# The high and low parts of a split input, moved into two regions of SBUF

## The chip, the cores and the metric

The kernel runs on one core of a Trainium2 chip. Its time is the device time of one execution in microseconds (us); lower is better. Five engines work beside each other in a core: TensorE (PE, matmuls; its weight loads are shown apart as PEld), VectorE (DVE), ScalarE (ACT), GpSimd (POOL) and SyncE (SP, which issues DMAs here). SBUF is the memory that they share, 128 partitions wide.

## The reference

Two blocks of a transformer over 256 tokens of width 1024, in float32. The first has two layers, each with a feed-forward part, an attention mixer, another feed-forward part and a gate; the second has a convolution and delta-rule mixer and 32 experts. The part that the change bears on is the input of the feed-forward parts and of two input products:

```python
def rms_norm(x, g):
    y = xf * lax.rsqrt(jnp.mean(xf * xf, axis=-1, keepdims=True) + EPS)
    return (y * g.astype(jnp.float32)).astype(x.dtype)

def swiglu(x, w_in, w_out):
    gate, up = jnp.split(x @ w_in, 2, axis=-1)
    return (jax.nn.silu(gate) * up) @ w_out

for i in range(DEPTH):                                     # DEPTH = 2
    h = h + FFN_HALF * swiglu(rms_norm(h, g_ffn1[i]), ffn1_w_in[i], ffn1_w_out[i])
    ...
    h = h + FFN_HALF * swiglu(rms_norm(h, g_ffn2[i]), ffn2_w_in[i], ffn2_w_out[i])
```

The hidden width of a feed-forward part is 2816, which is 22 chunks of 128.

## The kernel before

Features lie on the partitions: an activation of width 1024 is 8 tiles (index k) of 128 features by 256 tokens (T = 256). Weights stream in from HBM in chunks of 24 tiles of 128x128 through a ring of four buffers.

The dense products keep float32 accuracy with a faster type. Weights and inputs are each split into a high part, rounded to float32r, and a low part, the rest, and a product is three matmuls: high by high, high weights by low input, low weights by high input. ScalarE makes the high weights (`high`, or `high_first` for a stage's first chunk; L1563), VectorE the low ones (`ring_lo`, L2050). For the input, ScalarE writes `x_hi` (`x_high_pair`, L1574) and VectorE `x_lo` (`x_low_pair`, L2079), tile by tile, as soon as the residual stream `h` has its new value. Both are views of one tensor, `x_parts`:

```python
x_parts = inside(rounded_view("x_parts", [P, 2 * KD * T + LINE]), [P, KD, 2, T])
x_hi, x_lo = x_parts[:, :, 0, :], x_parts[:, :, 1, :]
```

In a partition the order is high k=0, low k=0, high k=1, low k=1 and so on, 256 elements each. `inside` starts a view 15 elements (INSIDE) into its tensor, which is 60 bytes behind a multiple of 64; every run of 256 elements of 4 bytes then starts at 60 bytes inside a group of 64. The tensor lies over `hn` and `sq`, which are used at other times. The hidden activations `act_hi` and `act_lo`, two tensors of their own, start 60 bytes inside as well.

Who reads `x_parts`:
- The four feed-forward stages (`gated`; `ffn1_0`, `ffn2_0`, `ffn1_1`, `ffn2_1`). For each of the 22 chunks, gate and up have 8 tiles each. Since high and low of one k are neighbours, one matmul of 512 columns multiplies a high weight with both and puts the results beside each other in a PSUM bank; one of 256 columns multiplies the low weight with `x_hi`. `gate_up` first issues the 16 of 512 columns and then the 16 of 256; `first_gate_up` goes by k, for the stage's first chunk, and waits for each k's low part. The down product of the chunk before, 24 matmuls of 256 columns from `act_hi` and `act_lo`, follows.
- The input product of the second block (`mix_in`): three matmuls of 256 columns for each tile, `x_hi` and then `x_lo` with the high weight, `x_hi` with the low one.
- The input product of the fox mixer (`two_units`), where 128 columns of `x_hi` or `x_lo` are the stationary operand and 512 columns of weights stream by.

All matmuls but the experts' go through the helper at L587. The order on TensorE is the order of the code; other engines are waited for by semaphores. The last quarter of the kernel, the experts, streams its weights from HBM and reads none of `x_parts`.

Of the kernel before, what the change touches and what calls it, by code (L numbers as in the profile page):

```python
# [14 lines left out]
P = 128  # L15
T = 256
D = 1024
KD = D // P
# [23 lines left out]
LINE = 16  # L42
INSIDE = 15
# [154 lines left out]
def two_block_kernel(nc, xT, pT, pos, par, weights, experts, out):  # L198
    with ExitStack() as ctx:
# [3 lines left out]
        def rounded_view(name, shape):  # L203

            with nc.sbuf_tensor("sb_" + name, shape, F32R) as view:
                return view

        def inside(flat, shape):

            n = math.prod(shape[1:])  # L210
            names = "abc"[:len(shape) - 1]
            dims = {a: shape[1 + i] for i, a in enumerate(names)}
            return flat[:, INSIDE:INSIDE + n].rearrange(f"p ({' '.join(names)}) -> p {' '.join(names)}", **dims)
# [23 lines left out]
        v_tok = sb("v_tok", [P, 2, D])  # L237
        oT = sb("oT", [P, KD, T])
        h = sb("h", [P, KD, T])
        x_parts = inside(rounded_view("x_parts", [P, 2 * KD * T + LINE]), [P, KD, 2, T])  # L240
        x_hi, x_lo = x_parts[:, :, 0, :], x_parts[:, :, 1, :]
        hn = sb("hn", [P, KD, T])
        sb("behind_hn", [P, LINE])
        sq = sb("sq", [P, KD, T])
# [338 lines left out]
        def _(pe):  # L583
# [92 lines left out]
            def gated(name):  # L676
# [3 lines left out]
                def product(bank, slot, part, k, inc=None):  # L680

                    w_hi, w_lo = split_tile(slot, 2 * k + part)
                    mm(bank[:, :], w_hi, x_parts[:, k, :, :].rearrange("p a t -> p (a t)"), k == 0, False)
                    mm(bank[:, 0:T], w_lo, x_hi[:, k, :], False, k == KD - 1, inc)

                def gate_up(slot, par):

                    banks = (GATE[par], UP[par])
                    for part, bank in enumerate(banks):
                        for k in range(KD):  # L690
                            w_hi, _ = split_tile(slot, part * KD + k)
                            mm(bank[:, :], w_hi, x_parts[:, k, :, :].rearrange("p a t -> p (a t)"), k == 0, False)
                    for part, bank in enumerate(banks):
                        for k in range(KD):
                            _, w_lo = split_tile(slot, part * KD + k)
                            mm(bank[:, 0:T], w_lo, x_hi[:, k, :], False, k == KD - 1,
                               gu_ready if part and k == KD - 1 else None)
# [2394 lines left out]
```

## Time and profile before

| | us |
|---|---|
| median of three executions | 1721.98 |
| lowest, highest | 1719.61, 1722.22 |
| the profiled execution | 1720.82 |
| its span, first to last instruction | 1719.0 |
| TensorE busy in the span | 1615.6 (94%) |
| VectorE, ScalarE, GpSimd busy | 987.5, 610.3, 57.4 |

The granted TensorE clock had a mean of 0.989 of full speed. A matmul's record ends some time after the next one has started, since matmuls are pipelined: the time that one takes of the engine is the distance from its start to the next one's, and not the mean duration in its row. Where a row merges several matmuls, the distance is the time from the row's start to the next row's, divided by their number.

### The profile page before, as it was taken

What the parts mean: (1) busy time and instruction counts of PE and PEld (TensorE: products, weight loads), DVE (VectorE), ACT (ScalarE), POOL (GpSimd) and SP (SyncE); (2) the same over time, 40 slices, a digit from 0 to 9 for tenths busy, and PEclk for the clock granted to TensorE, in tenths of its full rate; (3) what the DMA queues carried; (4) which work ended last, traced back from release to release, by engine and by line L of the source; (5) the groups of instructions that cost most, each with busy time, mean ns of one, the idle gap of its engine ahead of it and who ended that gap; (6) DMA issues with size and microseconds to landing.
All of it is one profiled execution on the core that took longest, in us unless ns stands there. A gap on an engine that the chain in (4) does not pass through costs nothing.

```text
span 1719.0 us, 25786 instructions
## 1 busy us (share of the span) xinstructions
PE 1615.6 (94%) x10376; PEld 1286.3 (75%) x10376; DVE 987.5 (57%) x1660; ACT 610.3 (36%) x809; POOL 57.4 (3%) x82
## 2 busy tenths in 40 slices
PE   7999999999999999999999999999989888788867
PEld 6999857899998999888889999999854444334423
DVE  7888655688767788865487885788331111111112
ACT  5333346434336333465543334653421000000001
POOL 4000005000000000001100000000000000000000
PEclk9999999999999999999999999999989999999999
DMA  7555442555554555544255555343699999999996
GB/s 282 191 183 183 184 184 74 184 184 188 194 232 160 195 198 190 190 153 173 74 191 195 197 187 212 120 147 124 240 375 426 426 426 427 428 427 428 427 427 245
DMA packets 49530, 415.68 MB, mean 242 GB/s; under 512 B 5648, under 2 KB 5680, under 8 KB 8368
## 3 DMA queue, kind: packets, MB, share of 16 engines
q1 hardware_dynamic: 49392, 414.61, 61.5%
q8 instruction: 53, 0.87, 0.2%
q14 instruction: 21, 0.17, 0.0%
q10 hardware_dynamic: 64, 0.03, 0.0%
HBM read 413.54 MB, written 1.05 MB: 241 GB/s over the span
## 4 chain that ended last, share of the span: by engine, by line
PE 74%; DMA 18%; DVE 4%; ACT 3%; issue 1%; SPq 0%; POOL 0%; DVEq 0%; ACTq 0%
PE bank L587 66%; DMA sb_moe_ring<-experts 17%; PE bank L1281 7%; DVE sb_ring_lo L2050 1%; ACT sb_high L1563 1%; DMA sb_ring<-weights 1%; PE bank L776 0%; PE bank L865 0%; DMA sb_h<-xT 0%; SPq L513 0%; DVE sb_x_parts L2079 0%; ACT sb_high_first L1563 0%; DVE sb_nmax L2183 0%; DVE sb_lnv L2086 0%; ACT sb_x_parts L1574 0%
## 5 line engine op out<-in xcount | busy, mean ns | idle before, releaser
L2050 DVE TENSOR_TENSOR sb_ring_lo<-sb_ring,sb_high 128x2304 fp32r<-128x2304 f32 (+4 forms) x180 | 351.9, 1956 | 123.5 <-ACT sb_high L1563 122.9
L587 PE MATMUL bank<-sb_x_parts,sb_high 128*128 128x512 f32 (+1 forms) x1792 | 407.5, 365 | 0.3 <-DVE sb_ring_lo L2050 0.2
L587 PEld LDWEIGHTS bank<-sb_x_parts,sb_high 128*128 128x128 f32 x1792 | 317.8, 189 | 49.4 <-DVE sb_ring_lo L2050 0.8
L1563 ACT ACTIVATE sb_high<-sb_ring 128x3072 fp32r<-128x3072 f32 x100 | 274.9, 2748 | 139.6 <-PE bank L587 111.0
L587 PE MATMUL bank<-sb_x_parts,sb_ring_lo 128*128 128x256 f32 x1632 | 253.0, 279 | 0.0
L587 PEld LDWEIGHTS bank<-sb_x_parts,sb_ring_lo 128*128 128x128 f32 x1632 | 224.5, 189 | 7.0
L587 PE MATMUL bank<-sb_act_hi,sb_ring_lo 128*128 128x256 f32 x704 | 195.0, 277 | 0.0
L587 PE MATMUL bank<-sb_act_hi,sb_high 128*128 128x256 f32 x680 | 188.6, 277 | 2.2 <-DVE sb_ring_lo L2050 1.7
L587 PE MATMUL bank<-sb_act_lo,sb_high 128*128 128x256 f32 x680 | 187.7, 276 | 0.0
L1605 ACT ACTIVATE sb_expg<-sb_gate_r 128x256 f32<-128x256 f32 x88 | 36.7, 418 | 338.0 <-DVE sb_gate_r L2113 337.9
L1281 PE MATMUL bank<-sb_moe_ring,sb_act 128*32 128x512 f32 x464 | 118.3, 640 | 38.1 <-DMA sb_moe_ring<-experts 38.1
L1281 PE MATMUL bank<-sb_moe_ring,sb_sq 128*32 128x512 f32 x960 | 115.5, 604 | 32.7 <-DMA sb_moe_ring<-experts 32.1
L587 PE MATMUL bank<-sb_oT,sb_ring 128*128 128x256 f32 x640 | 142.8, 379 | 0.0
L587 PEld LDWEIGHTS bank<-sb_oT,sb_ring 128*128 128x128 f32 x640 | 120.7, 190 | 16.7 <-issue 0.8
L587 PEld LDWEIGHTS bank<-sb_act_hi,sb_ring_lo 128*128 128x128 f32 x704 | 131.7, 187 | 0.0
L587 PEld LDWEIGHTS bank<-sb_act_hi,sb_high 128*128 128x128 f32 x680 | 127.2, 187 | 2.6 <-DVE sb_ring_lo L2050 1.9
L587 PEld LDWEIGHTS bank<-sb_act_lo,sb_high 128*128 128x128 f32 x680 | 127.2, 187 | 0.0
L1281 PEld LDWEIGHTS bank<-sb_moe_ring,sb_act 128*32 128x32 f32 x464 | 31.1, 116 | 108.9 <-issue 108.2
L2838 DVE TENSOR_TENSOR sb_act<-bank,sb_expg 128x128 f32<-128x128 f32 x32 | 9.3, 291 | 162.1 <-ACT sb_expg L1991 162.1
L1281 PEld LDWEIGHTS bank<-sb_moe_ring,sb_sq 128*32 128x32 f32 x960 | 27.8, 109 | 97.5 <-issue 94.0
L2833 DVE COPY sb_sq<-bank 128x512 f32<-128x512 f32 x32 | 22.1, 691 | 131.8 <-PE bank L1281 131.8
L1281 PEld LDWEIGHTS bank<-sb_stack,sb_sq 128*128 128x128 f32 x512 | 59.6, 191 | 29.7 <-issue 29.7
(395 smaller groups left out, 1922.7 us busy)
## 6 DMA issues: line engine op xcount, KB each, us to landing
sb_ring<-weights SPq DMA_DIRECT2D x133, 1536.0 KB, 6.5
sb_moe_ring<-experts SPq DMA_DIRECT2D x176, 1024.0 KB, 21.9
sb_qk<-experts SPq DMA_DIRECT2D x8, 1024.0 KB, 17.9
sb_front<-experts SPq DMA_DIRECT2D x2, 1024.0 KB, 13.2
sb_oT<-experts SPq DMA_DIRECT2D x2, 1024.0 KB, 17.6
sb_moe_ring<-experts SPq DMA_DIRECT2D x8, 256.0 KB, 19.1
sb_front<-experts SPq DMA_DIRECT2D x2, 768.0 KB, 14.2
sb_h<-xT SPq DMA_DIRECT2D x2, 512.0 KB, 6.6
```

Source lines behind the costliest of these rows:

```text
L587: ins = nc.tensor.matmul(o, l, r, start=start, stop=stop, skip_group_check=True)
L1281: ins = nc.tensor.matmul(o, l, r, start=start, stop=stop, skip_group_check=True)
L1563: nc.scalar.activation(high_of(n)[:, lo * P:hi * P], ring[:, n % RING, lo * P:hi * P], ACT.Copy).then_inc(done, 1)
L1605: nc.scalar.activation(expg[:, b, :], gate_r[:, b, :], ACT.Silu).then_inc(sig_ready, 1)
L2050: return V.tensor_tensor(ring_lo[:, n % RING, cols], ring[:, n % RING, cols], high_of(n)[:, cols].bitcast(F32), ALU.subtract)
L2833: V.tensor_copy(partial[:, 1, :], B[1][:, :]).then_inc(part_in[1], 1)
L2838: V.tensor_tensor(a3, turned_part(1), s3_, ALU.mult).then_inc(ex_act, 1)
```

## The change

High and low parts get a region each inside `x_parts`. The high region has the eight tiles of `x_hi` behind each other, starting at element 15; the low region has those of `x_lo`, starting at element 15 + 2049 = 2064 = 129 x 16, a multiple of 64 bytes. Two neighbours of one k are now 2049 elements apart. The matmuls of 512 columns read them as two runs of 256, [2049, 2] by [1, 256]; what they write in PSUM is the same 512 columns. The tensor is 16 elements longer. What ScalarE and VectorE write, and all waits, stay as they were; the number of instructions is the same on every engine.

```diff
-        x_parts = inside(rounded_view("x_parts", [P, 2 * KD * T + LINE]), [P, KD, 2, T])
-        x_hi, x_lo = x_parts[:, :, 0, :], x_parts[:, :, 1, :]
+        x_run = KD * T + LINE - INSIDE
+        x_both = rounded_view("x_parts", [P, 2 * KD * T + 2 * LINE])[:, INSIDE:INSIDE + 2 * x_run]
+        x_parts = x_both.rearrange("p (a n) -> p a n", a=2)[:, :, 0:KD * T].rearrange("p a (k t) -> p a k t", t=T)
+        x_hi, x_lo = x_parts[:, 0, :, :], x_parts[:, 1, :, :]
...
                 def product(bank, slot, part, k, inc=None):
-                    mm(bank[:, :], w_hi, x_parts[:, k, :, :].rearrange("p a t -> p (a t)"), k == 0, False)
+                    mm(bank[:, :].rearrange("p (a t) -> p a t", a=2), w_hi, x_parts[:, :, k, :], k == 0, False)
...
                 def gate_up(slot, par):
-                            mm(bank[:, :], w_hi, x_parts[:, k, :, :].rearrange("p a t -> p (a t)"), k == 0, False)
+                            mm(bank[:, :].rearrange("p (a t) -> p a t", a=2), w_hi, x_parts[:, :, k, :], k == 0, False)
```

## Rows read from the trace of the kernel before

**Rows 1.** Page: the span, TensorE's busy time, the chain's shares.

```profile
span 1719.0 us, 25786 instructions
...
PE 1615.6 (94%) x10376; PEld 1286.3 (75%) x10376; DVE 987.5 (57%) x1660; ACT 610.3 (36%) x809; POOL 57.4 (3%) x82
...
PE bank L587 66%; DMA sb_moe_ring<-experts 17%; PE bank L1281 7%; DVE sb_ring_lo L2050 1%; ACT sb_high L1563 1%; DMA sb_ring<-weights 1%; PE bank L776 0%; PE bank L865 0%; DMA sb_h<-xT 0%; SPq L513 0%; DVE sb_x_parts L2079 0%; ACT sb_high_first L1563 0%; DVE sb_nmax L2183 0%; DVE sb_lnv L2086 0%; ACT sb_x_parts L1574 0%
```

**Rows 2.** Windows: stretch, busy time and instructions by engine, granted clock, DMA.

```profile
546.00:706.00 160.00, 159.37 (x1071) 146.90 (x1071) 129.62 (x176) 62.37 (x44) 0.00 (x0) 1.00 0.51 188
...
865.00:1050.00 185.00, 184.81 (x1236) 170.30 (x1236) 146.65 (x202) 72.82 (x59) 0.00 (x0) 1.00 0.53 194
...
1093.00:1208.00 115.00, 115.00 (x958) 111.72 (x958) 97.58 (x161) 61.26 (x67) 0.00 (x0) 1.00 0.35 129
```

**Rows 3.** Waits of TensorE: who waited for whom, total us, times, longest.

```profile
PE bank L1281 <- DMA sb_moe_ring<-experts: 70.1, 42, 3.0
PE bank L587 <- DVE sb_ring_lo L2050: 13.6, 3, 11.7
```

**Rows 4.** Groups by shape, moving operand named first: busy us, mean ns of one.

```profile
L587 PE MATMUL bank<-sb_x_parts,sb_high 128*128 128x512 f32 x1344 | 322.4, 391 | 0.3 <-DVE sb_ring_lo L2050 0.2
...
L587 PE MATMUL bank<-sb_x_parts,sb_high 128*128 128x256 f32 x448 | 85.1, 288 | 0.1
...
L587 PE MATMUL bank<-sb_x_parts,sb_high_first 128*128 128x512 f32 x64 | 26.4, 445 | 11.8 <-DVE sb_ring_lo L2050 11.7
```

**Rows 5.** Timeline of TensorE, a turn of ffn1_1's loop: start us, us, operation.

```profile
603.70 0.28 PE L587 MATMUL bank<-sb_act_hi,sb_high 128*128 128x256 f32 x1
...
606.47 3.83 PE L587 MATMUL bank<-sb_x_parts,sb_high 128*128 128x512 f32 x16
610.14 2.03 PE L587 MATMUL bank<-sb_x_parts,sb_ring_lo 128*128 128x256 f32 x16
612.01 0.28 PE L587 MATMUL bank<-sb_act_hi,sb_high 128*128 128x256 f32 x1
...
614.78 3.83 PE L587 MATMUL bank<-sb_x_parts,sb_high 128*128 128x512 f32 x16
```

**Rows 6.** Timeline of TensorE in the fox mixer, weights as the moving operand.

```profile
759.33 0.39 PE L587 MATMUL bank<-sb_ring_lo,sb_x_parts 128*128 128x512 f32 x1
...
768.99 0.39 PE L587 MATMUL bank<-sb_ring_lo,sb_x_parts 128*128 128x512 f32 x1
```

**Rows 7.** Timeline in the attention, around the mask's matmul.

```profile
279.77 0.92 PE L587 MATMUL bank<-sb_qk 96*128 96x128 f32 x4
...
280.34 0.47 PE L587 MATMUL bank<-sb_mask_r,sb_ident_r 128*128 128x256 f32 x1
```

**Rows 8.** Timeline of the input product of the second block, 14 groups of three.

```profile
1130.77 0.28 PE L587 MATMUL bank<-sb_x_parts,sb_ring_lo 128*128 128x256 f32 x1
...
1135.71 0.28 PE L587 MATMUL bank<-sb_x_parts,sb_ring_lo 128*128 128x256 f32 x1
```

**Rows 9.** All that touches `x_parts`: ns min/median/max; who waited, us and times.

```profile
L587 PEld LDWEIGHTS bank<-sb_high,sb_x_parts x168: 187/187/192, 740.1 to 806.3; 128*128 128x128 f32 x168
...
  PEld bank L587: 1.0, 3
```

**Rows 10.** Writers of `x_parts` and the same operations into aligned tensors, by shape.

```profile
L1574 ACT ACTIVATE sb_x_parts<-sb_h,sb_params 128x256 fp32r<-128x256 f32 x48 | 21.2, 495 | 11.4 <-DMA sb_h<-xT 5.6 <-DVE sb_h L2043 3.5 <-DVE sb_h L2227 2.3
L1656 ACT ACTIVATE sb_oT<-sb_h,sb_params 128x256 f32<-128x256 f32 x16 | 6.6, 497 | 5.4 <-DVE sb_h L2043 5.4
...
L2079 DVE SCALAR_TENSOR_TENSOR sb_x_parts<-sb_h,sb_params,sb_x_parts 128x256 fp32r<-128x256 f32 x48 | 20.8, 479 | 12.5 <-ACT sb_x_parts L1574 12.5
L2515 DVE SCALAR_TENSOR_TENSOR sb_qk<-sb_attn,sb_params,sb_qk 128x256 f32<-128x256 f32 x36 | 15.9, 482 | 0.6
```

## The prediction, made before the changed kernel ran

> **What bounds the kernel now.** I read the header and the shares of the chain first, then the waits of TensorE, then the windows by stage, and only then single instructions. TensorE is busy 94% of a span of 1719.0 us, and 66% of the chain that ended last is one line, the helper L587 through which every product outside the experts goes [rows 1]. Between 546 and 706 us it is busy 159.37 of 160 us, between 865 and 1050 us 184.81 of 185, and in the mixer's input product 115.00 of 115 [rows 2]. So in the dense stages nothing is waited for: of all TensorE waits on L587 the largest is 13.6 us in three places, and they are waits for split weights, which the change doesn't touch [rows 3]. Behind the dense stages the chain is the experts' DMA (17% of it), which reads none of the inputs that move. The change gives TensorE no work and takes none; it alters where its streamed operand lies. Hence only one question carries the forecast: does the spacing of the matmuls that read the moved operand change, by how many ns, times how many of them.
>
> **How many.** Four feed-forward stages with 22 chunks of 16 products each: 4 x 22 x 16 = 1408 matmuls of 512 columns stream high and low in one instruction. The profile has all of them, 1344 against weights in the high buffers and 64 against the first chunks' [rows 4]. One nanosecond on each is 1.4 us. A difference of 0.2%, about what a measurement of this kernel can tell from no change, is 3.4 us, or 2.4 ns on each of the 1408. Besides these, 224 products of the mixer's input read the low part alone, as the second of three matmuls of 256 columns (448 with high weights, of which half read low), and the fox mixer has x as its stationary operand.
>
> **How fast they go now.** In one turn of the loop 16 such matmuls start at 606.47 and the next group at 610.14: 3.67 / 16 = 229.4 ns. The following 16 of 256 columns take (612.01 - 610.14) / 16 = 116.9 ns each, and the 24 of the down product (606.47 - 603.70) / 24 = 115.4 ns [rows 5]. The granted clock is 1.00 throughout, the upper level of 2.4 GHz [rows 2], so no part of this is the clock. All of these start 60 bytes inside a group of 64. For an aligned start there is a row too: in the fox stage weights stream and x is stationary, 42 matmuls of 512 columns in 768.99 - 759.33 = 9.66 us, 230.0 ns [rows 6]. The two kinds of start are 0.6 ns apart, and the aligned one is the slower. Where a run starts is thus a small thing here.
>
> **Part 1: the jump.** After the change the 512 columns are two runs of 256 with a step of 2049 elements between them. High ends after 15 elements of its last group, low begins a new one. Counted in groups of 64 bytes, before it was elements 15 to 526, 33 groups; now 15 to 270, 17 groups, plus 16 for low, 33 again. If what such a matmul pays beside its columns goes with groups, nothing changes. No row shows a jump between two runs of this size, so I bound it. From above: a jump can hardly cost more than ending one matmul and starting another, which is also a jump, and comes with a new weight load. Two matmuls of 256 columns take 2 x 116.9 = 233.8 ns or 2 x 115.4 = 230.8 ns against 229.4 in one, so 4.4 or 1.4 ns; x 1408 = 6.2 or 2.0 us [rows 5]. The only matmul that streams two runs is the mask's (2 x 128 columns, the same 128 twice, and a split output as well): the products ahead of it end at 279.77 + 0.92 = 280.69, it ends at 280.34 + 0.47 = 280.81, so about 120 ns for 256 columns [rows 7], within the rounding of these rows of the 115 to 117 without a jump. From below: the low run now starts on a group, which for a whole matmul is 0.6 ns slower, not faster; a gain would have to come from the parting of high and low, which is weighed as a rival below. I take the value nearest to a row of the same size, the aligned run's: + 0.6 ns x 1408 = + 0.8 us, and keep 0 to + 6.2 us.
>
> The Trainium skill ("TensorE: Matmul & The Clock Gate", Back-to-back issue gap) puts a fixed 2.5 ns on every matmul beside its columns. If a jump cost such a start, an estimate by that page is 1408 x 2.5 = + 3.5 us instead of + 0.8; the rows give 1.4 to 4.4 ns for a start here, so they agree in size, but neither says that a jump is one. For a whole matmul the page gives 512 / 2.4 + 2.5 = 215.7 ns, and the trace differs: 229.4. The skill ("SBUF — State Buffer", Door 1: The DMA port swizzle) also says that full bandwidth needs at least two hits on a 16-byte line, which would favour aligned starts; the rows disagree, 230.0 ns aligned against 229.4 ns 60 bytes in.
>
> **Part 2: low read alone.** The mixer's groups of three go at (1135.71 - 1130.77) / 14 = 352.9 ns [rows 8], the down product's, whose high and low lie in tensors far apart, at 8 groups in 2.77 us = 346.2 ns [rows 5]. The same three shapes, 6.6 ns apart. If that comes from high and low being 1024 bytes apart in one region, separate regions give 224 x 6.6 ns = 1.5 us back; if not, nothing, or the 0.6 ns of an aligned start, + 0.1 us. I take the middle, - 0.7 us.
>
> **Part 3: the fox mixer.** A third of its weight loads now read low from an aligned address. Those loads (187 ns each) [rows 9] lie beside 512 columns of 230.0 ns, so the stream sets the pace. Nothing; if the cover were gone I would see it in the 230.0.
>
> **Part 4: the writers.** ScalarE writes the high part, 48 times 495 ns at 60 bytes inside a group; the same operation and scale into an aligned tensor takes 497 ns. VectorE's low part takes 479 ns, its sister into an aligned tensor 482 [rows 10]. The low write gets aligned and high loses its gaps: at most 48 x 3 ns = 0.1 us, most of it behind TensorE. Where TensorE waited for the low part it was 1.0 us in three places [rows 9], so even there it is noise. No instruction, semaphore or DMA is added, so no queue gets anything new behind it. Nothing.
>
> **Sum.** + 0.8 - 0.7 = + 0.1 us against the profiled execution's own 1720.8 us (span 1719.0 and 1.8 around it). That execution is 1.2 us under the median of three, 1722.0, so the forecast is 1722.1 us; the three runs themselves reach from 1719.6 to 1722.2.
>
> **The rivals.**
> A jump is a start: the stream stops at the end of the high run and is set up again, 1.4 to 4.4 ns, middle 2.9, x 1408 = + 4.1 us, 1726.1 us (1724.0 to 1728.2). For it: such a price is what every matmul pays now. Against it: part of that price may be the weights' change, and the mask's row shows nothing of it. It decides the verdict from 2.4 ns a matmul on. This is the slower side.
> What costs the mixer 6.6 ns in each of its threes is that high and low are neighbours, and it is in the 512 columns too, which read the same neighbours: 6.6 ns x 1408 = - 9.3 us, 1712.7 us. For it: both read the same bytes. Against it: a stream of 512 weights without such neighbours goes no faster, 230.0 ns, and in the mixer the cost may lie in the change from one run to the other and not in either.
> Only the mixer gains: - 1.5 us and a free jump, 1720.5 us. It is a shade of the forecast and ends as no change.
> A jump costs much more than a start, over 5 ns, above 1729 us: for it only that no row has such a jump.
> That the change doesn't do what it says, say a matmul cut into two, can be left out: the program of the changed kernel has as many TensorE instructions as before, with the two runs as one operand.
>
> **How the numbers follow.** Forecast, with the shade: 0.62. A start per jump: 0.25, a fifth of it below the 3.4 us that can be told apart. A gain in the 512 columns: 0.09. Much more than a start: 0.04. Faster 0.09; slower 0.20 + 0.04 = 0.24; within 0.2%: 0.67. The range takes in the start per jump at its upper end, 1728.2, and below it the mixer's gain and the spread of the runs, to 1718.8.
>
> **What would show it.** In the changed profile: the group of x with high weights, 128x512, x1344, busy 322.4 us now. It is 84 groups of 16, so each ns of spacing adds 84 x 15 ns = 1.3 us to it: about 323 if I am right, 326 if a jump is a start, 314 if the neighbours were to blame. One loop turn is 8.31 us from 606.47 to 614.78 and should stay within 0.02; a start per jump makes it 8.36. The mixer's three should stand between 346 and 353 ns. The fox stage's 230.0 ns, the writers' 495 and 479 ns should stand still. If the span moves while all of these stand, my premise that only the spacing matters is wrong.

## The result and the profile after

The changed kernel takes 1723.1 us (median of 22 executions, 1720.95 to 1725.08), the kernel before 1720.6 us in the same sessions (22 executions, 1718.31 to 1723.19). The ratio is 1.0014, 95% interval 1.0007 to 1.002: 2.5 us slower. That is small but clear of the spread, and it stays within the 0.2% named in the prediction. The time forecast was 1722.1 us. The profiled execution of after took 1723.0 us with a span of 1721.3.

The page of after, header and busy times (compare [rows 1]; lines from the change on stand two further down, so L587 is now L589):

```profile
span 1721.3 us, 25786 instructions
...
PE 1620.0 (94%) x10376; PEld 1287.1 (75%) x10376; DVE 987.7 (57%) x1660; ACT 610.5 (35%) x809; POOL 57.3 (3%) x82
...
PE bank L589 66%; DMA sb_moe_ring<-experts 17%; PE bank L1283 7%; DVE sb_ring_lo L2052 1%; ACT sb_high L1565 1%; DMA sb_ring<-weights 1%; PE bank L778 0%; PE bank L867 0%; DMA sb_h<-xT 0%; SPq L515 0%; DVE sb_x_parts L2081 0%; ACT sb_high_first L1565 0%; DVE sb_nmax L2185 0%; DVE sb_lnv L2088 0%; ACT sb_x_parts L1576 0%
```

As many instructions and as many matmuls as before, but TensorE is busy 4.4 us longer (1615.6 to 1620.0), and the chain has the same shape. The stages are as gapless as in [rows 2], at the same granted clock of 1.00 (stretch, busy time and instructions by engine, clock, DMA):

```profile
546.00:706.00 160.00, 159.14 (x1057) 145.16 (x1057) 128.92 (x175) 63.59 (x45) 0.00 (x0) 1.00 0.52 192
865.00:1050.00 185.00, 184.77 (x1234) 168.94 (x1233) 146.69 (x203) 72.95 (x60) 0.00 (x0) 1.00 0.52 191
```

The groups by shape, busy us and mean ns of one, say which matmuls (compare [rows 4]; the second group, low weights by the high part of the input, was 253.0 us before):

```profile
L589 PE MATMUL bank<-sb_x_parts,sb_high 128*128 128x512 f32 x1344 | 324.7, 393 | 0.3 <-DVE sb_ring_lo L2052 0.2
L589 PE MATMUL bank<-sb_x_parts,sb_ring_lo 128*128 128x256 f32 x1632 | 254.4, 280 | 0.0
```

322.4 has become 324.7, about midway between the 323 of the forecast and the 326 of the rival "a jump is a start". The turn of the loop shows the spacing (TensorE's timeline: start us, us, operation; compare [rows 5]):

```profile
603.69 2.04 PE L589 MATMUL bank<-sb_x_parts,sb_ring_lo 128*128 128x256 f32 x16
605.57 0.28 PE L589 MATMUL bank<-sb_act_hi,sb_high 128*128 128x256 f32 x1
...
608.34 3.86 PE L589 MATMUL bank<-sb_x_parts,sb_high 128*128 128x512 f32 x16
612.04 2.04 PE L589 MATMUL bank<-sb_x_parts,sb_ring_lo 128*128 128x256 f32 x16
```

The 16 matmuls of 512 columns take 3.70 us, 231.3 ns each (229.4 before). The 16 of 256 columns take 605.57 - 603.69 = 1.88 us, 117.5 ns each (116.9 before). The down product, which reads other tensors, still takes 2.77 us. The turn is 8.35 us where it was 8.31; the prediction had named at most 0.02 us of change for the forecast and 8.36 us for a start per jump, so by this sign the trace stood nearer to the rival. Rows are rounded to 10 ns; the mean distance of starts over all such matmuls in the trace is finer, and is what the rest of this text uses where it gives hundredths:

| start to start, ns | before | after | difference x count |
|---|---|---|---|
| 512 columns, high weights | 229.56 | 231.21 | +1.65 x 1408 = +2.3 us |
| 256 columns, low weights | 116.61 | 117.54 | +0.93 x 1408 = +1.3 us |
| mixer, group of three | 353.1 | 353.6 | +0.5 x 224 = +0.1 us |
| fox mixer, weights stream | 230.2 | 231.1 | +1.0 x 288 = +0.3 us, not clear of the spread |
| down product | 115.56 | 115.55 | 0 |

The fox mixer's row is weak: two executions of one and the same kernel further down, in which `x_parts` lies as before, have 230.2 and 230.8 ns there. With it the sum is +4.0 us, without it +3.7. From the first matmul to the last of the second block's input product the profiles have 1202.1 us before and 1205.8 after, +3.7. Of that 0.45 lies ahead of the first down product, where the spacing explains less than 0.1 (32 matmuls of each kind), and the stretch from `ffn1_0` to `ffn2_0`, with the attention in it, gives 0.34 back. Apart from such shifts at the edges of stages, which the spacing doesn't explain, the dense part lost what the spacing says: 0.040 us in every turn of the loops. The medians of the whole kernel lie 2.5 us apart, with 3.4 as the upper end of their interval, and the profile of before spends 1.6 us more on the experts than that of after. That last difference is between two single executions and says nothing about the change.

### The profile page after: what moved, and what is told of

Read it like the earlier page. It is cut to its first block, busy times and chain, and to the rows that moved or that the text cites. A ratio compares the mean times of both kernels' runs of the same rounds, so it can differ in the third digit from the quotient of the medians.

```text
span 1721.3 us, 25786 instructions
## 1 busy us (share of the span) xinstructions
PE 1620.0 (94%) x10376; PEld 1287.1 (75%) x10376; DVE 987.7 (57%) x1660; ACT 610.5 (35%) x809; POOL 57.3 (3%) x82
## 4 chain that ended last, share of the span: by engine, by line
PE 74%; DMA 18%; DVE 4%; ACT 3%; issue 1%; SPq 0%; POOL 0%; DVEq 0%; ACTq 0%
PE bank L589 66%; DMA sb_moe_ring<-experts 17%; PE bank L1283 7%; DVE sb_ring_lo L2052 1%; ACT sb_high L1565 1%; DMA sb_ring<-weights 1%; PE bank L778 0%; PE bank L867 0%; DMA sb_h<-xT 0%; SPq L515 0%; DVE sb_x_parts L2081 0%; ACT sb_high_first L1565 0%; DVE sb_nmax L2185 0%; DVE sb_lnv L2088 0%; ACT sb_x_parts L1576 0%
## 5 line engine op out<-in xcount | busy, mean ns | idle before, releaser
L589 PE MATMUL bank<-sb_x_parts,sb_high 128*128 128x512 f32 (+1 forms) x1792 | 409.9, 367 | 0.3 <-DVE sb_ring_lo L2052 0.2
L589 PEld LDWEIGHTS bank<-sb_x_parts,sb_high 128*128 128x128 f32 x1792 | 316.5, 188 | 53.0 <-DVE sb_ring_lo L2052 0.7
L589 PE MATMUL bank<-sb_x_parts,sb_ring_lo 128*128 128x256 f32 x1632 | 254.4, 280 | 0.0
L589 PEld LDWEIGHTS bank<-sb_x_parts,sb_ring_lo 128*128 128x128 f32 x1632 | 225.3, 190 | 7.2
L589 PE MATMUL bank<-sb_act_hi,sb_ring_lo 128*128 128x256 f32 x704 | 195.2, 277 | 0.0
L589 PE MATMUL bank<-sb_act_hi,sb_high 128*128 128x256 f32 x680 | 188.7, 277 | 2.2 <-DVE sb_ring_lo L2052 1.7
L589 PE MATMUL bank<-sb_act_lo,sb_high 128*128 128x256 f32 x680 | 187.9, 276 | 0.0
L589 PE MATMUL bank<-sb_oT,sb_ring 128*128 128x256 f32 x640 | 142.8, 380 | 0.0
L589 PEld LDWEIGHTS bank<-sb_oT,sb_ring 128*128 128x128 f32 x640 | 120.9, 190 | 16.4 <-issue 0.8
L589 PEld LDWEIGHTS bank<-sb_act_hi,sb_ring_lo 128*128 128x128 f32 x704 | 131.9, 187 | 0.0
L589 PEld LDWEIGHTS bank<-sb_act_hi,sb_high 128*128 128x128 f32 x680 | 127.6, 188 | 2.5 <-DVE sb_ring_lo L2052 1.9
L589 PEld LDWEIGHTS bank<-sb_act_lo,sb_high 128*128 128x128 f32 x680 | 127.4, 187 | 0.0
```

The costliest lines, as they stand in the source:

```text
L589: ins = nc.tensor.matmul(o, l, r, start=start, stop=stop, skip_group_check=True)
```

## The experiments

Four kernels, the streams, leave out the whole computation and do nothing but matmuls: 64 on each line of code, 16 weight tiles in turn, moving operands at the places of the kernels, one line after the other with no wait. (In the lines of code shown, the last argument, the flags that begin and end a sum, is left out.) A line's start subtracted from the next line's, divided by 64, is the time of one matmul. The other eight are whole kernels.

### The layouts alone, nothing beside them

Among the lines of `e1_streams_quiet` (in the run all lines stood two further down than the text on record says, so "before" is L429 and so on):

```python
M(whole(i), W(i), one(15 + 512 * k))         # L429: before
M(split(i), W(i), two(15 + 256 * k, 2049))   # L430: after
M(split(i), W(i), two(15 + 256 * k, 2064))   # L431: both runs 60 bytes inside
M(whole(i), W(i), one(512 * k))              # L432: one run of 512, aligned
M(split(i), W(i), two(256 * k, 2064))        # L433: both runs aligned
M(whole(i), W(i), one(15 + 256 * k))         # L435: one run of 512, k 1024 bytes apart
M(whole(i), W(i), one(15))                   # L437: before, always one place
M(split(i), W(i), two(15, 2049))             # L438: after, always one place
M(half(i), L(i), one(15 + 512 * k, T))       # L439: 256 columns, before
M(half(i), L(i), one(15 + 256 * k, T))       # L440: 256 columns, after
```

> Leaves the whole computation out and only streams matmuls from the same addresses as the kernel, 64 of each kind on a line of its own, twice, while no other engine works; its time is no time of the kernel. What is read is the distance from one start to the next. L427 is the stream of before (512 contiguous, 60 bytes inside, k apart 2048 bytes), L428 that of after (two runs, low aligned), L429 two runs both 60 inside, L430 contiguous aligned, L431 two runs both aligned, L432 high aligned and low inside, L433 contiguous with k only 1024 bytes apart, L434 two runs one element apart, L435 and L436 before and after with the same addresses each time; L437 to L442 are 256 columns with the low weights: 2048 and 1024 bytes apart inside, the same aligned, always the same place inside, and the low region of after. Theory 1, a jump inside an instruction costs by itself: L428, L434 and L436 stand 1.5 ns or more above L427 and L435, L433 does not, and L437 and L438 are equal. Theory 2, what counts is how far successive matmuls read from each other (1024 bytes instead of 2048), jump or not: L433 stands above L427 and L438 0.9 ns above L437, and L436 equals L435. Theory 3, other engines' accesses collide with the new places: nothing differs here, all 512 streams within 0.5 ns of 229.6, all 256 ones of 116.6.

TensorE's timeline of this kernel:

```profile
39.90 14.86 PE L429 MATMUL bank<-sb_x_raw,sb_high 128*128 128x512 f32 x64
54.60 14.95 PE L430 MATMUL bank<-sb_x_raw,sb_high 128*128 128x512 f32 x64
69.39 14.88 PE L431 MATMUL bank<-sb_x_raw,sb_high 128*128 128x512 f32 x64
84.11 14.69 PE L432 MATMUL bank<-sb_x_raw,sb_high 128*128 128x512 f32 x64
98.64 15.08 PE L433 MATMUL bank<-sb_x_raw,sb_high 128*128 128x512 f32 x64
113.55 15.09 PE L434 MATMUL bank<-sb_x_raw,sb_high 128*128 128x512 f32 x64
128.49 14.67 PE L435 MATMUL bank<-sb_x_raw,sb_high 128*128 128x512 f32 x64
142.99 14.77 PE L436 MATMUL bank<-sb_x_raw,sb_high 128*128 128x512 f32 x64
157.61 14.68 PE L437 MATMUL bank<-sb_x_raw,sb_high 128*128 128x512 f32 x64
172.12 14.95 PE L438 MATMUL bank<-sb_x_raw,sb_high 128*128 128x512 f32 x64
186.91 7.63 PE L439 MATMUL bank<-sb_x_raw,sb_ring_lo 128*128 128x256 f32 x64
194.38 7.67 PE L440 MATMUL bank<-sb_x_raw,sb_ring_lo 128*128 128x256 f32 x64
```

Before: (54.60 - 39.90) / 64 = 229.7 ns. After: 14.79 / 64 = 231.1. The kernels' own numbers, with nothing else running. The 256 columns are there too: 116.7 ns on L439, and 117.4 on L440 (mean of its starts). So nothing else at work is needed for either difference. Two lines were a surprise: one run of 512 aligned takes 227.0 ns, and the layout of before read always at the same place (L437) takes 226.8, with k 1024 bytes apart (L435) 226.7. The latter refutes the second theory, that successive reads closer together cost more. At one place the two runs of after (L438) take 231.1, 4.3 ns more than one run. The layout of before thus has something that costs it 2.9 ns, and after has another cost. What before has and those have not: its matmuls lie end to end, so that each begins in the group of 64 bytes in which the one ahead of it ended. I call this the shared group. In 256 columns the roles are swapped: high tiles were 2048 bytes apart and are 1024 apart now, so after has the shared group and before has not.

### The same with ScalarE and VectorE at work

```diff
-        LOAD = 0
+        LOAD = 180
```

> The same streams as in the run before it, again with the computation left out, but ScalarE rounds a chunk of weights and VectorE subtracts one over and over beside them, as in the kernel's loop. Theories 1 and 2: the differences between the lines are those of the quiet run within 0.5 ns. Theory 3: L428 stands 1.5 ns above L427 and L438 0.9 above L437 here and only here.

The timeline and, below it, the window from 40 to 100 us (stretch, busy by engine, clock):

```profile
39.20 14.86 PE L429 MATMUL bank<-sb_x_raw,sb_high 128*128 128x512 f32 x64
53.89 14.95 PE L430 MATMUL bank<-sb_x_raw,sb_high 128*128 128x512 f32 x64
68.68 14.88 PE L431 MATMUL bank<-sb_x_raw,sb_high 128*128 128x512 f32 x64
```

```profile
40.00:100.00 60.00, 60.00 (x263) 49.12 (x262) 59.38 (x19) 59.30 (x23) 0.00 (x0) 1.00 0.00 1
```

VectorE and ScalarE are 99% busy on the same memory, and by the means of starts each of the lines keeps its time to 0.1 ns (229.6, 231.1 and 230.0 in both runs). That contention with the other engines' reads sets the spacing is refuted.

### Both parts 60 bytes inside, and one region aligned

The first is the change with the alignment of the low part taken back, the second the kernel before with its one region aligned:

```diff
-        x_run = KD * T + LINE - INSIDE
+        x_run = KD * T
-        x_both = rounded_view("x_parts", [P, 2 * KD * T + 2 * LINE])[:, INSIDE:INSIDE + 2 * x_run]
+        x_both = rounded_view("x_parts", [P, 2 * KD * T + LINE])[:, INSIDE:INSIDE + 2 * x_run]
```

> Two regions as in the changed kernel, but low starts 60 bytes inside a group too (step 2048 elements instead of 2049), so a jump stays and the streams touch 34 groups of 64 bytes instead of 33. If the jump costs as such: as the changed kernel, 1.0014 of before. If groups are what is paid for, about 0.4 ns a group more on 1408 matmuls, 0.6 us above the changed kernel, 1.0018. If the aligned start of low was the cost, back to before, 1.000.

```diff
-        x_parts = inside(rounded_view("x_parts", [P, 2 * KD * T + LINE]), [P, KD, 2, T])
+        x_parts = rounded_view("x_parts", [P, 2 * KD * T + LINE])[:, 0:2 * KD * T].rearrange("p (k a t) -> p k a t", k=KD, a=2)
```

> The kernel before with its one region moved to a multiple of 64, so no jump and no 60 bytes, all 512-column streams aligned. From the fox stage's 230.0 ns against 229.4: 0.6 ns on 1408 is 0.8 us, ratio 1.0005, if alignment is as small a thing as I took it for. If the 60 bytes are worth more, on 256 columns above all (1632 of them and 448), then 1 ns on each adds 2 us, 1.0015 to 1.002, and the loss of the changed kernel may be low's alignment.

Both parts inside: ratio 1.0008 [0.9999, 1.0017], 230.11 and 117.07 ns. One region aligned: 1.0011 [1.0002, 1.002], 228.2 and 119.5 ns, and the fox mixer's streams, whose stationary operand moved, go from 230.2 to 227.2. The first result lies between the outcomes named beforehand: by its time it can't be told from before or from after, by its spacing 512 columns pay 0.55 ns where after pays 1.65. In the second, 512 columns gain 1.4 ns and 256 columns lose 2.9, also in the mixer, where the group of three goes from 353.1 to 359.5 ns; there are more of the latter, and the kernel is slower than before. No single rule "aligned is better" or "inside is better" holds. The Trainium skill ("SBUF — State Buffer", Door 1: The DMA port swizzle) asks for at least two hits on a 16-byte line, which favours aligned starts. 256 columns disagree here. 512 columns seem to agree, but the next streams show that what they gain is the shared group: without it an aligned run takes 227.3 ns and one 60 bytes inside 226.7.

### The order in which the operands are read

If the shared group costs, reading k in the order 0 2 4 6 1 3 5 7 must take the cost away without moving a byte: no two successive matmuls are neighbours. First in streams (`R` is that order):

```python
M(whole(i), W(i), one(15 + 512 * k))          # L430: before
M(whole(i), W(i), one(15 + 512 * R[k]))       # L431: before, mixed order
M(whole(i), W(i), one(15 + 528 * k))          # L433: gaps of 64 bytes between them
M(whole(i), W(i), one(512 * R[k]))            # L434: aligned, mixed order
M(split(i), W(i), two(15 + 256 * R[k], 2049)) # L435: after, mixed order
M(whole(i), W(i), one(4))                     # L441: one place, 16 bytes inside
M(whole(i), V15(i), one(15 + 512 * R[k]))     # L448: as L431, weights 60 bytes inside
M(whole(i), V15(i), one(512 * R[k]))          # L449: as L434, weights 60 bytes inside
```

> Streams alone again, the computation left out, 64 matmuls a line. (In the two runs of streams before, every line stood two further down than expected: before's stream was L429, after's L430, and so on.) They showed 229.6 ns for before, 231.0 for after, but 226.8 when before's stream always reads the same place and 226.7 when its start moves by 1024 bytes. New theory, shared group: a matmul that begins in the group of 64 bytes in which the last one ended pays for it, 2.9 ns at 512 columns and 0.8 at 256; a jump inside an instruction costs some 4.3 ns besides. Rival, step: what costs is a start that moves by 2048 bytes. L430 before as it is, 229.6. L431 the same, k in the order 0 2 4 6 1 3 5 7: shared group 226.7, step 229 or more. L432 backwards, k = 7 to 0: shared group 226.7; step 229.6. L433 k apart 2112 bytes, no group shared: shared group 226.7, step 229.6. L434 aligned, mixed order, 226.7 either way. L435 after's stream in the mixed order: the jump remains, 231. L436 both regions aligned, 233. L437 256 columns 1024 bytes apart 117.4, L438 the same in mixed order 116.7 if it is the shared group, L439 1088 bytes apart 116.7. L440 to L443 512 columns from one place at 0, 16, 32, 48 bytes inside, L444 to L447 256 columns likewise: 226.7 for all of 512 and between 116.7 and 120 for 256. L448 to L451 with the weights 60 bytes inside too, for the stationary operand's place.

The timeline of this kernel:

```profile
40.60 14.86 PE L430 MATMUL bank<-sb_x_raw,sb_high 128*128 128x512 f32 x64
55.30 14.67 PE L431 MATMUL bank<-sb_x_raw,sb_high 128*128 128x512 f32 x64
69.81 14.67 PE L432 MATMUL bank<-sb_x_raw,sb_high 128*128 128x512 f32 x64
84.31 14.82 PE L433 MATMUL bank<-sb_x_raw,sb_high 128*128 128x512 f32 x64
98.97 14.71 PE L434 MATMUL bank<-sb_x_raw,sb_high 128*128 128x512 f32 x64
113.52 14.95 PE L435 MATMUL bank<-sb_x_raw,sb_high 128*128 128x512 f32 x64
128.31 15.07 PE L436 MATMUL bank<-sb_x_raw,sb_high 128*128 128x512 f32 x64
...
255.30 14.78 PE L448 MATMUL bank<-sb_x_raw,sb_high 128*128 128x512 f32 x64
269.92 14.89 PE L449 MATMUL bank<-sb_x_raw,sb_high 128*128 128x512 f32 x64
284.64 7.63 PE L450 MATMUL bank<-sb_x_raw,sb_high 128*128 128x256 f32 x64
```

L430 takes 229.7 ns, L431 in mixed order 14.51 / 64 = 226.7, L432 backwards the same. L435, after in mixed order, keeps its 231.1. In 256 columns 117.3 become 116.7. Those are hits. Two misses: gaps of 64 bytes (L433), where no group is shared, still take 229.1 where 226.7 was expected, and in 256 columns 118.0 where 116.7 was expected, more than with a shared group; and one fixed place takes 227.2, 231.6, 233.4 and 233.2 ns at 0, 16, 32 and 48 bytes inside a group (256 columns: 119.9, 118.8, 116.75, 118.3). The shared group is one case of something wider. The last lines are about the stationary operand: with it 60 bytes inside, an aligned stream takes 14.72 / 64 = 230.0 ns (L449) instead of 227.3 (L434), the two numbers of the fox mixer. That mixer's 230 ns are thus the price of where its stationary operand lies.

Then in the kernels themselves:

```diff
+SPREAD = (0, 2, 4, 6, 1, 3, 5, 7)
...
                     for part, bank in enumerate(banks):
-                        for k in range(KD):
+                        for k in SPREAD:
                             w_hi, _ = split_tile(slot, part * KD + k)
```

> The kernel before, its 16 matmuls of 512 columns in each chunk taken in the order k = 0 2 4 6 1 3 5 7 in place of 0 to 7; nothing moves in memory. Shared group: 2.9 ns less on 84 x 16 of them, 1344 x 2.9 = 3.9 us, ratio 0.9977 of before, the 512 group busy near 318.7 us. Step: no change, 1.000. A jump that costs by itself says nothing of this kernel.

For the changed kernel the same, in the series of low weights as well:

> The changed kernel, both its series of 16 in the mixed order. Shared group: the 256-column ones come back from 117.5 to 116.7 ns, 1344 x 0.8 = 1.1 us less than the changed kernel, while the 512 ones keep the jump at 231.2; ratio about 1.0008 of before. If the order helped the 512 ones here as well, it would be 0.998 or less, and the jump would not be what they pay for.

The groups by shape of before in mixed order, and of after in mixed order:

```profile
L588 PE MATMUL bank<-sb_x_parts,sb_high 128*128 128x512 f32 x1344 | 318.8, 388 | 0.4 <-DVE sb_ring_lo L2051 0.4
```

```profile
L590 PE MATMUL bank<-sb_x_parts,sb_high 128*128 128x512 f32 x1344 | 324.6, 393 | 0.3 <-DVE sb_ring_lo L2053 0.2
L590 PE MATMUL bank<-sb_x_parts,sb_ring_lo 128*128 128x256 f32 x1632 | 253.5, 280 | 0.0
```

Before drops from 322.4 to 318.8 (226.98 ns each), the number expected; the whole kernel gets faster than both others, 0.9985 [0.9976, 0.9994], 1717.4 us against 1720.3. After keeps its 512 columns (231.21) and gets two thirds of its loss in 256 columns back (117.54 to 116.92). Its ratio stays 1.0014 [1.0005, 1.0023] where about 1.0008 was expected, a miss in time: the dense stretch of its profile is 1.0 us shorter than that of after, which the medians don't resolve. With the same order and no shared group on either side only the layout is left between these two kernels: 231.21 - 226.98 = 4.2 ns is what the jump to the low region costs.

### Where the gain of the mixed order went

1408 x 2.58 ns is 3.6 us, but the medians were 2.8 us apart, and a repetition had less still:

> The kernel before with the mixed order alone, once more, beside the one with the low part first: 0.9985 again, between 0.9976 and 0.9994 as measured, and 226.98 ns a matmul.

It measured 0.999 [0.9981, 0.9999], 1.6 us by the medians. The traces tell why. Here is by how much each kernel's down products start earlier than those of before at the same place in the program, in us:

| start in before, us | mixed order | repetition | what lies behind it |
|---|---|---|---|
| 26.5 | 0.40 | -0.64 | start of the first loop |
| 199.2 | 1.16 | 0.10 | `ffn1_0` |
| 333.3 | 1.44 | 0.19 | attention |
| 720.1 | 3.10 | 1.83 | `ffn2_0` and `ffn1_1` |
| 727.6 | 1.44 | 0.18 | last chunk of `ffn1_1`, fox mixer's first products |
| 872.4 | 1.76 | -0.10 | fox mixer |
| 1044.2 | 2.56 | 0.70 | `ffn2_1` |

In the loops the lead grows by 0.04 us a turn, 16 x 2.58 ns, everywhere. Then 1.65 us are lost within 8 us, in both executions. TensorE's timeline there, first before, then the mixed order:

```profile
724.76 0.38 PE L587 MATMUL bank<-sb_act_hi,sb_high 128*128 128x256 f32 x1 [1.75 <-DVE sb_ring_lo L2050]
724.99 0.28 PE L587 MATMUL bank<-sb_act_lo,sb_high 128*128 128x256 f32 x1
725.10 0.28 PE L587 MATMUL bank<-sb_act_hi,sb_ring_lo 128*128 128x256 f32 x1
```

```profile
721.77 0.40 PE L588 MATMUL bank<-sb_act_hi,sb_high 128*128 128x256 f32 x1 [1.85 <-DVE sb_ring_lo L2051]
721.99 0.39 PE L588 MATMUL bank<-sb_act_lo,sb_high 128*128 128x256 f32 x1
...
725.38 0.30 PE L588 MATMUL bank<-sb_act_hi,sb_ring_lo 128*128 128x256 f32 x1
```

And 3.65 us behind the wait in both (the number behind POOL is the granted clock), before and then the mixed order; TensorE gets through 29 matmuls in the one and 18 in the other:

```profile
724.75:728.40 3.65, 3.64 (x29) 3.49 (x29) 2.62 (x5) 1.71 (x4) 0.00 (x0) 1.00 1.00 414
```

```profile
721.75:725.40 3.65, 3.63 (x18) 3.63 (x19) 1.54 (x3) 1.03 (x3) 0.00 (x0) 0.54 1.01 417
```

Here TensorE waits for a split weight in each kernel. The faster loop comes to it a little earlier, and waits 1.85 us instead of 1.75. Behind that wait 17 matmuls take (725.38 - 721.77) / 17 = 212 ns each instead of 116 (the granted clock is at its lower level, 1.2 GHz): 17 x 96 ns = 1.6 us. The clock fell behind waits of 1.85, 1.84 and 1.85 us in the three executions of the mixed order that were profiled, and not behind those of 1.51 to 1.75 us in the seven other whole kernels of this text, before and after among them. That the longer wait is the cause is a correlation over ten executions; no kernel changed the wait alone. 3.6 - 1.65 = 2.0 us is what is left of the gain, between the two measured 2.8 and 1.6. That the repetition began 0.64 us behind, where the first execution was 0.40 ahead, is a shift of the start that no matmul of this text explains.

### How far the jump counts

Both regions aligned, the low one 2064 elements behind the high one, which is 64 bytes more than a multiple of 256 bytes:

```diff
-        x_run = KD * T + LINE - INSIDE
+        x_run = KD * T + LINE
-        x_both = rounded_view("x_parts", [P, 2 * KD * T + 2 * LINE])[:, INSIDE:INSIDE + 2 * x_run]
+        x_both = rounded_view("x_parts", [P, 2 * KD * T + 2 * LINE])[:, 0:2 * x_run]
```

> Two regions, both at a multiple of 64. From the streams alone: 512 columns with a jump between two aligned runs 233.1 ns, 256 aligned 120.0. Against before that is 3.5 x 1408 + 3.4 x 1408 = 9.7 us, plus up to 3 ns on the 672 matmuls of the mixer, 2.0 us: ratio 1.0055 to 1.007. If the jump's price did not depend on where the runs lie, only the second half, 1.003.

1.0062 [1.0047, 1.0078] with four executions, 1731.2 us: the slowest layout of all, 232.73 and 119.6 ns. Both numbers hit: the streams had foretold them.

The streams with jumps of many sizes from a high run 60 bytes inside (`two(at, step)` reads 256 elements at `at` and 256 at `at + step`):

```python
M(whole(i), W(i), one(15))         # L430: one run of 512
M(split(i), W(i), two(15, 257))    # L431: low aligned, one element skipped
M(split(i), W(i), two(15, 273))    # L432: the same, 64 bytes further
M(split(i), W(i), two(15, 289))    # L433: 128 bytes further
M(split(i), W(i), two(15, 305))    # L434: 192 bytes further
M(split(i), W(i), two(15, 321))    # L435: 256 bytes further
M(split(i), W(i), two(0, 272))     # L446: both aligned
M(split(i), W(i), two(0, 2048))    # L447: both aligned
```

> Streams alone, the computation left out, 512 columns and always the same place unless said. L430 contiguous, 226.8. L431 to L442 two runs, high 60 bytes inside, low on a group, the step between them 257, 273, 289, 305, 321, 385, 513, 1025, 2049, 2065, 2081, 3073 elements. If a jump to the very next group is no jump (the run before with a gap of one element showed 228.4, the contiguous stream with the same steps of k 229.2): L431 is 226.8 and all others 231. If distance counts, the price grows from L432 to L442. If the parity of the group counts (high ends in an even one, a natural successor is odd), L432, L434 and L440 stand apart from L431, L433, L439. L443 to L445 low inside as well, steps 272, 2048, 2064: near 230. L446 and L447 both aligned, steps 272 and 2048: 233 if it is the alignment, less at 2048 if it was parity. L448 contiguous with k 2176 bytes apart: 226.7 if parity of the start explains why 2112 bytes cost 229.2; L449 and L450 two places in turn, 2112 and 2048 bytes apart; L451 2112 bytes in the mixed order, all for the same question.

The timeline of this kernel:

```profile
39.91 14.67 PE L430 MATMUL bank<-sb_x_raw,sb_high 128*128 128x512 f32 x64
54.42 14.95 PE L431 MATMUL bank<-sb_x_raw,sb_high 128*128 128x512 f32 x64
69.21 15.09 PE L432 MATMUL bank<-sb_x_raw,sb_high 128*128 128x512 f32 x64
84.14 15.09 PE L433 MATMUL bank<-sb_x_raw,sb_high 128*128 128x512 f32 x64
99.07 14.88 PE L434 MATMUL bank<-sb_x_raw,sb_high 128*128 128x512 f32 x64
113.79 14.96 PE L435 MATMUL bank<-sb_x_raw,sb_high 128*128 128x512 f32 x64
128.58 14.96 PE L436 MATMUL bank<-sb_x_raw,sb_high 128*128 128x512 f32 x64
...
276.56 15.09 PE L446 MATMUL bank<-sb_x_raw,sb_high 128*128 128x512 f32 x64
291.49 14.71 PE L447 MATMUL bank<-sb_x_raw,sb_high 128*128 128x512 f32 x64
306.04 14.98 PE L448 MATMUL bank<-sb_x_raw,sb_high 128*128 128x512 f32 x64
```

One run: 226.7 ns. Steps of 257, 273, 289 and 305 elements: 231.1, 233.3, 233.3, 230.0; then 321, 385, 513, 1025, 2049 and 3073 elements all 231.1, and 2065 and 2081 again 233.3. The cost repeats every 256 bytes, and the distance plays no part. A single skipped element costs as much as 12 KB, which was a miss: 226.8 was expected for it. Both aligned, a step of 272 takes 233.3 ns and one of 2048 takes 227.3, where one aligned run of 512 at one place had 227.2: there a jump over a whole region is free. So not the jump costs, but the place within 256 bytes at which the next run begins. This is no full rule: with the low run 60 bytes inside as well (L443 to L445), steps of 272, 2048 and 2064 elements all take 230.0 to 230.1 ns, whatever their place. And single runs 2176 bytes apart (L448), for which 226.7 was expected, take 231.6. This gave the last test, in which the slow kernel with both regions aligned differs in 16 elements of step:

```diff
-        x_run = KD * T + LINE
+        x_run = KD * T
```

> Two regions, both aligned, as in the run that gave 1.0062, but low 2048 elements behind high in place of 2064, so one group of 64 bytes nearer. The streams alone say that a jump is free when it lands where the next group of the run would have been within a stretch of 256 bytes (aligned, step 2048: 227.3 ns; step 2064 or 272: 233 ns), and costs 3 to 6 ns where it doesn't. Place within 256 bytes: the 512-column matmuls fall from 232.7 to about 227.5 ns, 1344 x 5.2 = 7.0 us less, ratio 1.0015 to 1.0025 of before, what remains being the aligned 256-column ones at 119.6. A jump costs as such: still 232.7 and 1.006.

The groups by shape, first of the kernel with both regions aligned, then of this one:

```profile
L589 PE MATMUL bank<-sb_x_parts,sb_high 128*128 128x512 f32 x1344 | 326.8, 395 | 0.2 <-DVE sb_ring_lo L2052 0.2
```

```profile
L589 PE MATMUL bank<-sb_x_parts,sb_high 128*128 128x512 f32 x1344 | 320.4, 390 | 0.3 <-DVE sb_ring_lo L2052 0.2
```

326.8 becomes 320.4 us (232.73 to 228.2 ns, what one aligned region has), and the ratio is 1.0016 [1.0007, 1.0025] instead of 1.0062. For aligned runs the place within 256 bytes is confirmed in the kernel.

### The mixer's groups of three

The mixed order in the loops, and in the mixer the low input first, so that no group is shared there:

```diff
+            def low_first(o, l, r, start, stop, inc=None):
+                mm(o, l[0], r[1], start, False)
+                mm(o, l[0], r[0], False, False)
+                mm(o, l[1], r[0], False, stop, inc)
...
-                        three(bank[:, j * T:(j + 1) * T], tl.next(), split_x(k), k == 0, k == KD - 1,
+                        low_first(bank[:, j * T:(j + 1) * T], tl.next(), split_x(k), k == 0, k == KD - 1,
```

> The kernel before with the mixed order in the feed-forward series and, in the second block's input product, each group of three taken as low, high, high instead of high, low, high, so that none begins where the last one ended. Shared group: three there go from 353.1 to about 350 ns, 192 x 3 = 0.6 us less than the mixed order alone, ratio 0.998. If only distance in memory counts, no difference from the mixed order alone.

The three go from 353.1 to 350.1 ns (116.62 + 116.68 + 116.80), which is 0.58 us over the 192 that the edit reaches. The whole kernel has 0.9986 [0.9977, 0.9995], 1718.0 against 1720.2 us, which can't be told from the mixed order alone.

### Spacing against time

The stretch from the first matmul to the last of the mixer's input product, against the 1202.1 us of before, beside the difference of the medians. The turn is that of a whole loop: 24 matmuls of the down product, 16 of 512 columns and 16 of 256; there are 84 groups of 16 and 16.

| kernel | 512 columns, ns | 256 columns, ns | down product, ns | turn, ns | stretch, us | medians, us |
|---|---|---|---|---|---|---|
| before | 229.56 | 116.61 | 2773.4 | 8313.4 | | |
| after | 231.21 | 117.54 | 2773.3 | 8353.4 | +3.7 | +2.5 |
| after, mixed order | 231.21 | 116.92 | 2776.5 | 8346.5 | +2.7 | +2.8 |
| both inside | 230.11 | 117.07 | 2792.5 | 8346.7 | +2.2 | +2.1 |
| one region, aligned | 228.2 | 119.5 | 2785.0 | 8346.7 | +2.1 | +2.1 |
| both aligned, 2064 elements apart | 232.73 | 119.6 | 2801.5 | 8445.7 | +10.7 | +10.9 |
| both aligned, 2048 elements apart | 228.2 | 119.5 | 2785.0 | 8346.6 | +2.4 | +2.9 |
| mixed order, two executions | 227.0 | 116.6 | 2776.7 | 8273.3 | -2.7, -1.5 | -2.8, -1.6 |
| mixed order, low first in the mixer | 227.0 | 116.6 | 2776.7 | 8273.3 | -2.7 | -2.3 |

The difference of the turn times 84 is +3.4 us for after, +2.8 for the four in the middle that have 8346.6, +11.1 for the slowest and -3.4 for the mixed order. With the 1.65 us of the lower clock added to the mixed ones, that lies within 1.0 us of every stretch. The rest is at the edges of stages and in the two mixers: ahead of the first down product alone, counted from their first matmuls, the kernels are between 0.7 us ahead of before and 0.5 us behind it. So the spacing of the loops explains the sign and the size of these times, but not every tenth.

Two things in this table are not explained. The down product reads `act_hi` and `act_lo`, which no edit touched, and still takes up to 28 ns more: about the first eight of its matmuls stand further apart, up to 10 ns. A matmul's distance thus carries something of the ones ahead of it. And four kernels with quite different splits have the same turn to 0.2 ns, so the parts of a turn are not prices that add up one by one.

## Why the prediction was right

**What bounds the kernel** was right. Only the spacing moved; writers (496 and 480 ns, [rows 10]), waits and clock stood still between before and after, and time went where TensorE streams the moved operand.

**Part 1, the jump,** forecast at +0.8 us, was +2.3 us: the direction and the order of size were right, the term was mis-sized by a factor of three, and its working was wrong in both halves. The count of groups of 64 bytes (33 and 33) does not price a matmul. The 0.6 ns, taken from the fox mixer's aligned stream [rows 6], was no price of alignment: that stream changed by 3 ns when its stationary operand moved, and one aligned run in the feed-forward's place takes 227.0 ns in the stream and 228.2 in the kernel, less than before. What the 1.65 ns are made of is a jump to a place that costs 4.2 ns (the two kernels in mixed order), less 2.6 ns for the shared group, which the new layout doesn't have.

**The 256 columns with low weights** were not in the sum at all. The prediction asked which matmuls read the moved operand low, and took those that read only high as unmoved. But high tiles moved together, 2048 bytes apart to 1024, and 0.93 ns on 1408 matmuls is +1.3 us, more than the whole of part 1 as forecast. [rows 5] had their 116.9 ns, and the step "how many" left them out.

**Part 2, the mixer,** forecast at -0.7 us, was +0.1. The gap between it and the down product [rows 5, 8] is real (353.1 and 346.7 ns by the finer means), and about half is the shared group (350.1 when avoided). The change doesn't avoid it: high k follows high k - 1 now, where low k followed high k. What the other 3.4 ns are is open.

**Part 3, the fox mixer,** forecast at nothing, was at most +0.3 us, and two executions of one kernel differ by nearly as much. "The stream sets the pace" holds, but the pace hangs on where the stationary operand lies: 227.2 ns with the input aligned, 230.2 before. **Part 4** was right.

**The rivals.** "A jump is a start" had the right sign, and its 2.9 ns lie between the net 1.65 and the 4.2 of the jump; its mechanism fell, since a jump of 2048 elements between aligned runs costs 0.1 ns. It was given a chance of 0.25 with an upper end of 1728.2 us. "What costs is that high and low are neighbours" was wrong for high and low within one matmul but near the truth for successive ones, and was worth 3.6 us and not 9.3. The forecast of +0.1 us thus came out as +2.5 by one term too small, one missed and one with the wrong sign. The range held it, because its ends were made from the rows of whole matmuls. In part that is luck: the term that was missed could have been as large as the 2.9 ns that alignment costs 256 columns, and the spacings by themselves add up to 3.7 us, just over the 3.4 that the prediction took for no change. What was right by its reasons is that only the spacing moved, and that a jump costs no more than the upper price of a start, 4.4 ns, against 4.2 measured.

## What to carry over

Where a kernel is bound by back-to-back matmuls, list every matmul that reads a moved tensor, also those whose own bytes look unmoved, and those that stand right behind one, and ask for each two things: where each of its runs begins within 256 bytes, and where the matmul ahead of it ended. The places tried here give no rule that covers all of them, so a new layout wants a stream of its own before it goes into the kernel. Before a layout is changed, try another order of the same reads: it costs nothing, and here it gave 0.15% (0.1% in the repetition) where the new layout cost 0.14%. Look at the waits behind a loop that gets faster: one that is 0.1 us longer may end with the clock at its lower level.

## What was not expected of the hardware

- The time of one matmul hangs on the start of its moving operand, with fresh weights each time: 512 columns take 226.7 ns (order or place without a shared group), 229.6 (end to end, 60 bytes inside) and up to 233.4 (one place, 32 bytes inside); 256 columns take 116.7 to 120.0. At one fixed place 60 bytes inside is as good as any for both (116.75 and 226.8); 32 bytes inside is as good for 256 columns (116.75) and the worst for 512 (233.4); 0 bytes is the worst for 256 (119.9).
- From a run 60 bytes inside to an aligned one, the cost of the second run repeats every 256 bytes: steps of 257, 273, 289 and 305 elements take 231.1, 233.3, 233.3 and 230.0 ns, and of these the first comes back up to 3073 elements, the second and third at 2065 and 2081; the fourth was tried once. To a second run 60 bytes inside it is 230.0 to 230.1 at three places.
- The stationary operand's place counts too: aligned streams of 512 columns take 227.3 ns with aligned weights and 230.0 with weights 60 bytes inside, in the streams as in the fox mixer (227.2 and 230.2).
- Matmuls that read unmoved tensors change their distance when they stand right behind moved ones, by up to 28 ns over a down product of 24.
- The Trainium skill ("TensorE: Matmul & The Clock Gate", Back-to-back issue gap) gives a single matmul 2.5 ns beside its columns, 512 / 2.4 + 2.5 = 215.7 ns. The fastest 512 columns in any run here take 226.7, 13.4 ns beside the 213.3 of the columns alone, and 256 columns 116.7, 10.0 ns beside 106.7. The trace differs from the page, and a part of the gap depends on addresses.
- ScalarE and VectorE at 99% beside TensorE change the spacing of the streams by less than 0.1 ns.
- What within the chip has these 64 and 256 bytes was not found; the streams give the times, not the unit that sets them.
